# GLA sample states in three pair buffers, their tail pieces regrouped, and the turned values copied ahead of a weight split

## The reference

```
def gla_step(q, k, v, log_a, S):
    def step(S, xs):
        qt, kt, vt, at = xs
        S = jnp.exp(at)[..., None] * S + kt[..., None] * vt[..., None, :]
        return S, jnp.einsum('bhk,bhkv->bhv', qt, S)
...
    if prompt:
        o, S = gla_chunked(q, k, v, log_a)
    else:
        o, S = gla_step(q, k, v, log_a, gla_state)
```

## Time and profile before

| what | value |
|---|---|
| median of 3 runs | 2705.14 us (2703.39 to 2705.47) |
| the profiled execution | 2697.52 us |
| its span | 2695.9 us |
| PE busy | 2595.8 us (96%) |
| DVE busy | 1549.1 us (57%) |
| ACT busy | 1233.5 us (46%) |
| POOL busy | 196.6 us (7%) |

### The profile page before, as it was taken

One profiled execution on the slowest core, in us unless ns is written; L12 is line 12 of the kernel. 1 busy time (PEld: TensorE's weight loads), 2 busy tenths in 40 slices (PEclk: granted clock), 3 DMA queues, 4 the chain that ended last, 5 costly groups with the idle time before them and its releaser, 6 DMA issues. The chain is left out here.

```text
span 2695.9 us, 52549 instructions
## 1 busy us (share of the span) xinstructions
PE 2595.8 (96%) x20839; PEld 2500.5 (93%) x20839; DVE 1549.1 (57%) x1943; ACT 1233.5 (46%) x1551; POOL 196.6 (7%) x307
## 2 busy tenths in 40 slices
PE   7999999999999999999999999998999999999997
PEld 5988888999999999999999988888899999999997
DVE  4556455444555555545644556455766665666666
ACT  5455554433443444433333534334555555455553
POOL 1111112000111111100000001310000000000000
PEclk9999999999999999999999999999999999999999
DMA  6778779666888888866657745855366567666563
GB/s 197 219 243 251 233 234 297 177 178 176 233 235 235 234 234 233 222 175 191 172 160 210 210 125 174 275 177 173 101 180 179 164 183 201 179 177 178 164 182 114
DMA packets 855041, 530.81 MB, mean 197 GB/s; under 512 B 13961, under 2 KB 832065, under 8 KB 854135
## 3 DMA queue, kind: packets, MB, share of 16 engines
q1 hardware_dynamic: 822583, 440.07, 59.4%
q0 software_dynamic: 27312, 86.50, 9.3%
q10 hardware_dynamic: 5032, 2.62, 0.3%
HBM read 499.79 MB, written 33.29 MB: 198 GB/s over the span
## 5 line engine op out<-in xcount | busy, mean ns | idle before, releaser
L520 DVE TENSOR_TENSOR weights_lo<-weights_raw,weights_hi 128x2048 fp32r<-128x2048 f32 x407 | 932.2, 2291 | 763.9 <-ACT weights_hi L513 762.0
L544 PE MATMUL bank<-h_hi,weights_hi 128*128 128x264 f32 x4624 | 1335.7, 289 | 18.9 <-DVE h_lo L2542 11.4
L545 PE MATMUL bank<-h_lo,weights_hi 128*128 128x264 f32 x4624 | 1316.6, 285 | 0.0
L546 PE MATMUL bank<-h_hi,weights_lo 128*128 128x264 f32 x4624 | 1315.1, 284 | 0.0
L544 PEld LDWEIGHTS bank<-h_hi,weights_hi 128*128 128x128 f32 x4624 | 876.6, 190 | 36.8 <-issue 22.8
L545 PEld LDWEIGHTS bank<-h_lo,weights_hi 128*128 128x128 f32 x4624 | 877.8, 190 | 2.0 <-issue 1.9
L513 ACT ACTIVATE weights_hi<-weights_raw 128x2048 fp32r<-128x2048 f32 x407 | 777.2, 1910 | 216.8 <-PE bank L546 207.2
L546 PEld LDWEIGHTS bank<-h_hi,weights_lo 128*128 128x128 f32 x4624 | 873.3, 189 | 0.0
L544 PE MATMUL bank<-y_hi,weights_hi 128*128 128x264 f32 x1232 | 353.5, 287 | 7.4 <-DVE y_lo L2450 3.8
L546 PE MATMUL bank<-y_hi,weights_lo 128*128 128x264 f32 x1232 | 352.1, 286 | 0.0
L545 PE MATMUL bank<-y_lo,weights_hi 128*128 128x264 f32 x1232 | 350.6, 285 | 0.0
(11 more groups left out here) (377 smaller groups left out, 2213.3 us busy)
## 6 DMA issues: line engine op xcount, KB each, us to landing
weights_raw<-in_w_in SPq DMA_DIRECT2D x177, 1024.0 KB, 7.0
weights_raw<-in_w_up SPq DMA_DIRECT2D x88, 1024.0 KB, 5.9
weights_raw<-in_w_down SPq DMA_DIRECT2D x64, 704.0 KB, 4.8
gla_state_sample<-in_state_gla POOLq DMA_DIRECT2D x32, 512.0 KB, 6.6
out_gla_s<-gla_state_sample POOLq DMA_DIRECT2D x32, 512.0 KB, 6.5
weights_raw<-in_w_br_gla SPq DMA_DIRECT2D x16, 1024.0 KB, 5.9
weights_raw<-in_w_mix_out SPq DMA_DIRECT2D x16, 1024.0 KB, 5.8
weights_raw<-in_w_xkv SPq DMA_DIRECT2D x16, 1024.0 KB, 6.0
```

The costliest lines, as they stand in the source:

```text
L520: nc.vector.tensor_tensor(w_lo[:, r, :], raw[:, r, :], w_hi[:, r, :].bitcast(F32), ALU.subtract).then_inc(lo_ready, 1)
L544: nc.tensor.matmul(out, wh, xh, start=first and n == 0, stop=False)
L545: nc.tensor.matmul(out, wh, xl, start=False, stop=False)
L546: mm = nc.tensor.matmul(out, wl, xh, start=False, stop=last and n == len(blocks) - 1)
```

## The change

There are six state buffers instead of four: samples 4 and 5 get their own, in rows 12 to 15 of `y_hi` and of `y_lo`. Samples 6 and 7 use those of samples 0 and 1. POOL's `gla_head` loads three pairs, the first before it waits for the values to be stored. The spread of values is a function of its own (`v_spread`); spreads 2 and 3 follow the stores of pairs 0 and 1 in `gla_tail`, and the load of pair 3 comes after the second of them. Semaphores for loaded and stored are three each, and waits are counted accordingly. ACT waits for the store of pair 2 before it writes `y_hi` of head 3. The table of pieces becomes two, two, one, one, two samples. On DVE the two copies of the turned values stand ahead of the weight split behind slot 8.

```diff
-        g_Ss = [at(f"gla_state_sample{r}", [P, 2, 512], (R_X + 8448 if r < 2 else R_M) + 4096 * (r % 2))
-                for r in range(4)]
+        g_Ss = [at(f"gla_state_sample{r}", [P, 2, 512], off) for r, off in enumerate(
+            (R_X + 8448, R_X + 12544, R_M, R_M + 4096, R_YH + 12 * TB, R_YL + 12 * TB))]
...
-        TAIL_SEQS = [(0, 1), (2, 3), (), (4, 5), (6, 7)]
+        TAIL_SEQS = [(0, 1), (2, 3), (4,), (5,), (6, 7)]
+
+        def pair_state(b):
+
+            return g_Ss[b % 6]
...
-        ss_in = [sem(f"gla_sample_state{r}_loaded") for r in range(2)]
-        ss_out = [sem(f"gla_sample_state{r}_stored") for r in range(2)]
+        ss_in = [sem(f"gla_sample_state{r}_loaded") for r in range(3)]
+        ss_out = [sem(f"gla_sample_state{r}_stored") for r in range(3)]
+
+        def state_count(q, h):
+
+            return h * 64 + 16 * (2 + 2 * (q == 3)) if q % 3 == 0 else h * 32 + 32
...
-                    for r in range(2):
-                        wait_loop(pool, (ss_out[r], h * 64))
+                    for q in range(3):
+                        wait_loop(pool, (ss_out[q], state_count(3 if q == 0 else q, h - 1)))
                 wait_loop(pool, A_GLA.at("vs", h))
                 pool.dma_start(d_vs[ds(h, 1)].rearrange("a b v -> (a b) v"), g_vs[:, :]).then_inc(vs_stored, 16)
-                for q in range(2):
+                for q in range(3):
                     ss_load(h, q)
+                    if q < 2:
+                        v_spread(h, q)
...
             def ss_load(h, q):
 
+                if q < 3:
+                    wait_loop(pool, P_GT.at(f"os{7 if q == 0 else 2 * q + 1}", h - 1))
+                else:
+                    wait_loop(pool, P_GT.at("os1", h), (ss_out[0], state_count(0, h)))
+                for b in (2 * q, 2 * q + 1):
+                    pool.dma_start(pair_state(b)[:, :, :], states("state_gla", h, b)).then_inc(ss_in[q % 3], 16)
+
+            def v_spread(h, q):
+
                 r = q % 2
                 if q < 2:
-                    wait_loop(pool, P_GT.at(f"os{2 * q + 5}", h - 1), (vs_stored, h * 16 + 16))
+                    wait_loop(pool, (vs_stored, h * 16 + 16))
                 else:
-                    wait_loop(pool, P_GT.at(f"os{2 * q - 3}", h), (ss_out[r], h * 64 + 32))
-                for b in (2 * q, 2 * q + 1):
-                    pool.dma_start(g_Ss[b % 4][:, :, :], states("state_gla", h, b)).then_inc(ss_in[r], 16)
+                    wait_loop(pool, V_GT.at(f"sn{2 * q - 3}_1", h))
...
                 for q in range(4):
                     wait_loop(pool, V_GT.at(f"sn{2 * q + 1}_1", h))
                     for b in (2 * q, 2 * q + 1):
-                        pool.dma_start(states("gla_s", h, b), g_Ss[b % 4][:, :, :]).then_inc(ss_out[q % 2], 16)
+                        pool.dma_start(states("gla_s", h, b), pair_state(b)[:, :, :]).then_inc(ss_out[q % 3], 16)
                     if q < 2:
-                        ss_load(h, q + 2)
+                        v_spread(h, q + 2)
+                    if q == 1:
+                        ss_load(h, 3)
...
-                        act.wait_ge(ss_in[b // 2 % 2], h * 64 + (b // 4 * 32 + 32))
+                        act.wait_ge(ss_in[b // 2 % 3], state_count(b // 2, h))
...
                 if k == 8:
                     act.wait_ge(*V_GT.at("osr", h))
+                    if isinstance(h, int):
+                        act.wait_ge(ss_out[2], state_count(2, h))
...
-                    split_lo(dve, p, j, h)
                     if j == 8:
                         for m in range(2):
                             dve.wait_ge(*P_GLA.at(f"t_v{m}", h))
                             nc.vector.tensor_copy(g_vtok[:, m, :], bank[6 + m][:, :]).then_inc(V_GLA(f"vtok{m}"), 1)
+                    split_lo(dve, p, j, h)
                     tail(j)
...
-            dve.wait_ge(ss_out[1], 4 * 64)
+            dve.wait_ge(ss_out[1], state_count(1, 3))
+            dve.wait_ge(ss_out[0], state_count(3, 3))
```

More of the change, by code:

```diff
@@ L829, in _ @@
             gla_tail(3)
-            for r in range(2):
-                pool.wait_ge(ss_out[r], 4 * 64)
+            for q in range(3):
+                pool.wait_ge(ss_out[q], state_count(3 if q == 0 else q, 3))
             pool.wait_ge(S_stored, 4 * 16)
@@ L1056, in gla_tail @@
                     for b in TAIL_SEQS[k]:
-                        act.wait_ge(ss_in[b // 2 % 2], h * 64 + (b // 4 * 32 + 32))
+                        act.wait_ge(ss_in[b // 2 % 3], state_count(b // 2, h))
                         for t in range(2):
-                            st = g_Ss[b % 4][:, t, :]
+                            st = pair_state(b)[:, t, :]
                             nc.scalar.activation(st, st, ACT.Copy, scale=la[:, ds(h * 2 + t, 1), NP + b])\
@@ L1603, in gla_tail @@
                             r = 32 * (2 * (b % 2) + t)
-                            mm = nc.tensor.matmul(bank[5][r:r + NS, :], g_qm[:, t, b, :], g_Ss[b % 4][:, t, :],
+                            mm = nc.tensor.matmul(bank[5][r:r + NS, :], g_qm[:, t, b, :], pair_state(b)[:, t, :],
                                                   start=b < 2, stop=b >= NS - 2)
```

## The result

The changed kernel takes 2674.22 us in the median of 4 runs (2673.47 to 2674.28), the kernel before 2704.26 us (2700.52 to 2705.47, 4 runs). The ratio is 0.9891, with a 95% interval of 0.9877 to 0.9905: 30.0 us less, where 16.7 were forecast and the range ended at 2681 us. The profiled execution took 2674.28 us, with a span of 2672.6 us, which is 23.3 us less than the span of before. In a later session, on chip 1, the kernel before took 2697.8 us (21 runs, 2693.98 to 2707.51) and the changed one 2676.9 us (5 runs, 2676.25 to 2678.18): 20.9 us less, ratio 0.9916 (0.9901 to 0.9931). The record doesn't say which chip the first result comes from.

A forecast was written before the change was run, and what follows sets the result against it. PE, busy 2595.8 of 2695.9 us, was taken as the bound, so only its waits mattered. 9.3 + 4.1 - 0.3 + 1.1 - 0.4 + 2.9 = 16.7 us off 2705.1 gave 2688.4 us, range 2681 to 2697.

The forecast's parts named there:

- waits at the states: PE's waits at L1604 for DVE's update of a sample's GLA state: 15.6 us, falling to about 5.3 us.
- chain behind slot 4: ACT split, ACT decay, DVE update for samples 6 and 7: ends at 273.4, just before PE arrives at 273.5.
- rival (a): GLA tails: samples 6 and 7 still come one behind the other; 6.5 us of gain lost, 2695 us; chance 0.16.
- (b): GLA tails: pair 3's load still lands after ACT wants it; 3.6 us gain left, 2701.5 us, or no change; chance 0.07.
- (c): Behind slot 3: sample 4's values land late and PE stalls, making the kernel slower, such as 2712 us; chance 0.05.
- term 3: Behind slot 8, turned values copied before the weight split: PE's 0.97 us waits in heads 1 to 3 go, 2.9 us.
- Term 2: Tail pieces two, two, one, one, two: waits after slot 4 go, 1.1 us gain; extra piece costs 0.4 us.
- term 1: Tails, three pair buffers, last pair loaded early: late waits go, 9.3 us; samples 6 and 7 overlap, 4.1 less 0.3.
- I carry the difference over to the median: Whole kernel: median 2705.14 us, 7.6 above the profiled execution; the 16.7 us gain was subtracted from the median.

The follow-up runs named there:

- load_late: Changed kernel with the load of pair 3 issued after the store of pair 2 instead of pair 1; 2708.0 us, ratio 1.0028 to the kernel before.
- copies_undone: Changed kernel with the copies of the turned values behind the weight split again; median 2682.6 us.
- old_pieces: Changed kernel with the earlier table of pieces (two, two, none, two, two); 2677.0 us against 2676.9 for the changed kernel in the same session.
- stall_filled: load_late with nine extra matmuls on PE ahead of sample 6 in each tail, adding nothing to the result; 2696.8 us.
- before_again: The kernel before, profiled a second time without an edit; GLA stage 445.9 us from the gate setup, against 442.5 in the first profile.
- before_third: The kernel before, profiled a third time without an edit; GLA stage 446.1 us from the gate setup, against 442.5 in the first profile.
- copies_only: Kernel before with only the two copies of turned values moved ahead of the weight split; 2696.2 us against 2697.8, ratio 0.9990.
- pairs_early: Changed kernel with samples 4 and 5 both behind slot 3 and none behind slot 4; median 2677.2 us.
- pairs_late: Changed kernel with no sample behind slot 1 and whole pairs behind slots 2 to 5; median 2679.5 us.
- pairs_late_load_first: pairs_late with POOL issuing the last values' spread and pair 3's load ahead of pair 1's store; 2671.0 us, ratio 0.9900 to the kernel before.

## Why the prediction was wrong

The 30.0 us are made up exactly, by the profiles and the runs of the first session: 18.1 us in the GLA stage, 7.5 behind it, 2.3 lost ahead of it, and 6.7 because the profile of the kernel before lay that far below its median of four while the changed kernel's lay at its own. Forecast were the first of these, at 16.7 us, and nothing for the others.

**Right: the waits that go, and what makes them go.** The waits at the states fell by 10.6 us (forecast 10.4), those at the turned values by 2.9, and samples 6 and 7 run side by side in all four tails. The chain behind slot 4 has the margin of 0.1 us that was worked out, and it held, so rival (a) did not come; with a margin that thin, luck had a part in it. Rivals (b) and (c) did not come either: the load of pair 3 is in place before ACT wants it, and sample 4 comes without a wait. In load_late the mechanism of (b) was made on purpose, and there the kernel became slower than the one before, where (b) had 3.6 us of gain left: the stalls are longer than those of before (4.5 to 5.4 us), and the clock fell behind each.

**Mis-sized: term 3.** I booked 2.9 us, the length of three waits, and nothing for head 0. Against copies_undone it is 4.0 us. Term 2 was booked at 1.1 us of gain and 0.4 of cost; against old_pieces it is 0.4 us, from 1.3 of gain and some 0.9 of cost. Together with term 1 the stage came out 1.4 us above the forecast, which alone would have stayed inside the range.

**Wrong: the step from the profile to the median.** "I carry the difference over to the median", "with PE's work the same": the kernel before had its profile 7.6 us below its median, and I took these 7.6 us as something that the changed kernel would have as well, with 2 us of scatter for the range. The changed kernel's profile lies at its median. The profiled execution of before was one in which the clock did not fall behind the stalls of some 2 us; in the two others it did, and their stage took 3.3 and 3.6 us more. With the stalls gone, this goes too: from 408.3 and 408.6 us to 386.9 is a gain of 21.5, not 18.1. A price for it was missing in term 1: a wait of PE was costed at its length, while load_late and stall_filled show 1.7 us more for each one that brings the clock down. That the unprofiled runs of the first session, which make its median, had such falls is not shown; if they had two each, that is about half of the 7.6 us.

**Wrong: that nothing else can move.** The range had no term for the part behind the stage. The same matmuls took from 2190.3 to 2200.9 us in the 14 profiles of the study, much of it by where the clock falls; between the two first profiles this gave 7.5 us, of which 2.7 are the pooling stage. In the mean of three profiles each, the stage gives 20.4 us and the part behind it 4.4, and 1.9 are lost ahead of the stage: 22.9 us, where the medians on chip 1 lie 20.9 and 22.4 us apart (2697.8 to 2676.9, and 2698.2 to 2675.8). The 30.0 us of the first session are more than this explains: its runs of the kernel before lay at 2700.5 to 2705.5, and no profile of such a run was taken.

Two smaller readings were off. The prediction says that a weight load beside the state loads runs at half its rate at worst, "as the 5.6 us and 13.2 us of rows 7 bear out"; 13.2 is 2.4 times 5.6, so these rows show more than a halving. Nothing hung on it. And the load of pair 3 was placed at about 255; it was issued at 250.69.

**What stays open.** Why the clock falls at one wait and not at another of the same length, and so whether the changed kernel's 4.4 us behind the stage (three profiles each) come with the change or by chance: the variants lie on both sides. No run says why the code ahead of the first `gla_q` x `gla_k` takes 91.8 to 92.3 us in the changed kernel, 90.0 to 90.1 in the one before and 90.3 to 91.4 in the variants.

## What to carry to other kernels

A stall of the engine that bounds the kernel can cost more than its length: a little more by itself, and a good deal more when the clock falls behind it. A single profile can be one in which it did not, so look at the granted clock, and compare the profiled execution with the median of the runs, before a profile's span is taken for the kernel's time. The scatter of the runs is not a sign to go by: it shrank from the kernel before (8.7 us in 10 runs of before_again) to the changed one (1.9 us in 5, 3.1 in 4), but load_late, with a fall in every tail, spans 4.1 us, and stall_filled and copies_undone, with none in the stage, 6.3 and 8.7 us. When two kernels are compared by stages, cut where both are in the same state: a cut inside a stretch of low clock hid 0.4 to 0.7 us here and would have turned the verdict on term 2. Where several small pieces hang on one chain of two other engines, moving a piece shifts the moment when the last one is wanted: count the end of the chain again after every move, and load what comes last ahead of a store that nobody waits for.

## What the runs showed of the hardware

- Waits of PE of 1.9 to 2.5 us brought the granted clock down in two of four tails (before_again, before_third), in three of four (copies_only) or in none (the first profile, with one of 2.96 us among them); waits of 4.5 to 5.4 us did so in four of four (load_late).
- Such a fall cost 1.7 us on PE's way in the GLA stage (418.2 against 411.5 us, four places). Matmuls put into the gap kept the clock up. At one wait of 2.81 us that all profiles share, the next 200 matmuls took 25.5 us without a fall, and 26.8 or 28.2 us with one.
- A wait of 0.97 us delayed PE by some 1.24 us with the clock at its upper level (390.9 against 386.9 us, three waits of this length and 0.35 us elsewhere).
- Two samples' products into different groups of output rows take 1.04 us together and 1.03 us alone, but only if the second is ready when the first starts: 2.12 us when its first matmul started 1.08 us later (pairs_early).
- A state load of 1 MB behind a store of 1 MB in the same queue landed after 10.6 us (pairs_late); issued ahead of it, it was there within 8.5 us and no longer waited for (pairs_late_load_first). In the changed kernel the landings of these loads reach 12.0 us, where 9.5 was the longest before.
